# A float32 mixture-of-experts tail on one core: the second gather moved into its own position, the last group moved behind the branch, and two gathers done in four column groups

## The chip, the cores and the metric

One core of a Trainium2 chip runs the whole program, one launch. The metric is the device time of one execution in microseconds, as the median of the runs; lower is better. Everything is computed in float32 (the matmuls of the expert part are plain float32).

## The reference, cut to what matters

Two layers of a diffusion backbone over 256 latent and 256 context tokens of width 1024. The last sub-layer of the second layer is the part at issue: a mixture of eight experts, each token using the best two.

```python
logits = (hf @ w_r).astype(jnp.float32) + b_r          # hf: 256 tokens x 1024
top_v, top_i = lax.top_k(logits, TOP_K)                # TOP_K = 2 of 8
gates = jax.nn.softmax(top_v, axis=-1)
combine = jnp.sum(one_hot(top_i, N_EXPERTS) * gates[..., None], axis=-2)
for e in range(N_EXPERTS):                             # w1, w3: 1024 x 2816, w2: 2816 x 1024
    out = out + combine[:, e:e + 1] * ((silu(hf @ w1[e]) * (hf @ w3[e])) @ w2[e])
```

Then comes the residual and a final RMSNorm.

## The kernel before, in words

**Positions, steps and units.** The eight experts are handled one after the other, in eight positions. Position 0 always holds expert 0; the others are filled with experts by their number of tokens, so which expert's weights a position loads is read from a register (line 588). Positions 1, 3, 5 and 7 (SMALL) work on two blocks of 32 token slots, the others on three. Each position is three steps (CH = 3, `g = 3 * e + j`), which cover 1024, 1024 and 768 of the 2816 hidden columns; there are NG = 24 steps. In step g TensorE does four pairs of first products (`pair(g, p)`, line 1172: two of the eight k tiles each, line 1187 issues the matmuls), turns the activations of step g-1 (`turn`, line 1158, lines 1164 and 1169) after its first pair, and ends with the second products of step g-1 (`second_unit`, line 1121, lines 1145 and 1153), one for each 256 hidden rows. The 32 token slots of a block are the columns of the loaded operand, so four such matmuls stand side by side in the array (four column groups of 32).

**The weight ring.** SyncE issues one DMA for each unit of weights, in the order in which TensorE uses them (lines 568 to 606, the DMA is line 575): a unit is 1 MB, or 768 KB for the first products of the third step of a position. The ring holds 16 units. Unit v is issued once `unit_done` says that unit v-16 has been used; a pair releases its two units with its last matmuls, each second product releases one. TensorE waits on a unit's arrival (`landed_unit`, line 1076).

**Gathers.** Before a position can run, the rows of its tokens are picked out of the 256 token rows `h2_rows` by products with 0/1 matrices that VectorE writes (`select`, line 2193). `gather(r, turn, i_, ps)` (line 1079, matmuls on line 1088) does one call: for turns 0 and 1 two k tiles, 96 slots each, two matmuls each with a full 128x128 loaded operand, so four matmuls a call and four calls a turn. ScalarE copies each call's bank to `held` (`gathered_rows`, line 1628, the copy is line 1633). Turn 0 serves position 0, turn 1 position 1, turn 2 positions 2 and 3, turn 3 the rest. Turn 0's four calls run back to back ahead of step 0 (lines 1197 and 1198). FILL_STEPS (line 71) says where the calls of the others go: turn 1's after the pairs (1,0), (1,1), (2,0) and (2,1), so inside position 0, turn 2's and turn 3's inside positions 1 and 3. In step 3 (ROW_STEP), the first of position 1, TensorE also turns the residual rows (`gate_rows`, `residual_rows`, lines 1092 to 1105), one after each pair, and VectorE copies them out (`rows_copied`, line 2233).

**The branch.** All of this is round 0. At its end every engine reads the largest number of tokens of an expert and branches (`rounds`, lines 534 to 547): only if some expert has more than 96 tokens do further rounds run. In TensorE's program the branch stands after the second products of step 22; behind it `last_scatter` (line 1238) does the three second products of step 23 and the scatter to token order (line 1118), and then VectorE and ScalarE do the final norm and SyncE stores.

```python
v = UNITS * r + H_UNIT[g, p, m]
load(v, unit(v, w), of_expert(name, e)...)      # unit v waits for unit_done >= v - 15
```

Of the kernel before, what the change touches and what calls it, by code (L numbers as in the profile page):

```python
# [11 lines left out]
P = 128  # L12
D = 1024
KT = D // P
# [44 lines left out]
CH = 3  # L59
WIDTH = [1024, 1024, 768]  # L60
NG = NE * CH
# [6 lines left out]
PLACE = [3, 4, 5, 6, 1, 2, 3, 0]  # L68
GATHERS = [(0,), (1,), (2, 3), (7, 4, 5, 6)]
FILL_ROWS = [2, 2, 2, 1]  # L70
FILL_STEPS = [None, [(1, 0), (1, 1), (2, 0), (2, 1)], [(4, 0), (4, 1), (5, 0), (5, 1)],
              [(g, p) for g in (10, 11) for p in range(4)]]
FIRST_FILL = [0, 4, 8, 12]
FILLS = 21
# [62 lines left out]
def backbone(nc, t, out):  # L137
    with ExitStack() as ctx:
# [46 lines left out]
        bank = [ctx.enter_context(nc.psum_tensor(f"bank{i}", [P, 512], F32)) for i in range(8)]  # L185
# [319 lines left out]
        def fill_of(turn, i, r):  # L505

            return FILLS * r + FIRST_FILL[turn] + i

        def fills_at(g, spot):

            return [(turn, FILL_STEPS[turn].index((g, spot))) for turn in (1, 2, 3) if (g, spot) in FILL_STEPS[turn]]

        def fill_sums(g, spot):

# [1 line left out]

        FIRST_FILL_BANK = [7, 6, 5, 3]
        ROW_STEP = CH
        ROW_BANK = [5, 2, 5, 2, 5]
        SCATTER_BANK = [0, 1, 2, 5]  # L520

        def kept_before(i, r):
# [98 lines left out]
        def _(pe):  # L621
# [457 lines left out]
            def gather(r, turn, i_, ps):  # L1079

                pe.wait_ge(sel_ready, SELECTS * r + turn + 1)
                cols = C * len(GATHERS[turn])
                for c in range(FILL_ROWS[turn]):
                    k = FILL_ROWS[turn] * i_ + c
                    if r + turn == 0:
                        pe.wait_ge(tok_ready, 2 if k < KT // 2 else 4)
                    for n in range(2):
                        i = mm(ps[:, c * cols:(c + 1) * cols], h2_rows[:, n, k * P:(k + 1) * P], sel_at[turn][n],
                               start=(n == 0), stop=(n == 1))
                i.then_inc(gather_mm, 1)  # L1090

            def residual_rows(pr):

                half, n = divmod(pr, 2)
                for c in range(4):
                    i = pe.transpose(bank[ROW_BANK[pr + 1]][:, c * P:(c + 1) * P], xv[:, 4 * half + c, n * P:(n + 1) * P], ident)
                i.then_inc(row_mm, 1)
# [56 lines left out]
                                   start=first, stop=last)  # L1154
                i.then_inc(unit_done, 1)

            def experts(r):
                def turn(g):

                    s01, s2 = sums(g, 0), sums(g, 1)  # L1160
                    nq = chunk_width(g) // P
                    pe.wait_ge(a_tok, before_group(g, r, 2, 3) + 2)
                    for q in range(nq):
                        i = pe.transpose(s01[:, q * P:(q + 1) * P], act_01[:, q * P:(q + 1) * P], ident)  # L1164
                    i.then_inc(a_mm, 1)
                    if g // CH not in SMALL:
                        pe.wait_ge(a_tok, before_group(g, r, 2, 3) + 3)
                        for q in range(nq):
                            i = pe.transpose(s2[:, q * HD:(q + 1) * HD], act_2[:, q * P:(q + 1) * P], ident[0:HD, 0:HD])
                        i.then_inc(a_mm, 1)  # L1170

                def pair(g, p):
                    e = g // CH
                    cw = chunk_width(g)
                    v3, v1 = UNITS * r + H_UNIT[g, p, 0], UNITS * r + H_UNIT[g, p, 1]
                    w3, w1 = unit(v3, 2 * cw), unit(v1, 2 * cw)
                    landed_unit(v3)
                    landed_unit(v1)
                    for kk in range(2):
                        k = 2 * p + kk  # L1180
                        for b in BLOCK_ORDER[e]:
                            ps = sums(g, b)
                            last = b == BLOCK_ORDER[e][-1]
                            for job in range(4):
                                w = w1 if (job < 2) == (b == 1) else w3
                                a = job % 2
                                i = mm(ps[BLOCK * job:BLOCK * (job + 1), 0:cw], gathered_block(e, k, b),  # L1187
                                       w[:, kk, a * cw:(a + 1) * cw], start=(k == 0), stop=(k == KT - 1))
                                if kk == 1 and last and a == 1:
                                    i.then_inc(unit_done, 1)  # L1190
                            if k == KT - 1 and not last:
                                i.then_inc(h_done, 1)

                if r:
                    pe.wait_ge(yt_ready, before(0, r, 1, 2))
                    pe.wait_ge(scatter_added, 4 * r)
                for i_ in range(4):
                    gather(r, 0, i_, bank[FIRST_FILL_BANK[i_]])
                for g in range(NG):
                    e, j = divmod(g, CH)  # L1200
                    for turn_ in (1, 2, 3):
                        if g in [step + 1 for step, _ in FILL_STEPS[turn_]]:
                            done = [step < g for step, _ in FILL_STEPS[turn_]].count(True)
                            pe.wait_ge(gathered, fill_of(turn_, done, r))
                    if g == 1 and r == 0:
                        pe.wait_ge(pos_ready, 2)
                    if g == ROW_STEP + 1 and r == 0:
                        pe.wait_ge(row_copied, 5)
                    if g == NG - 1:
                        pe.wait_ge(gathered, FILLS * (r + 1))  # L1210
                    for p in range(KT // 2):
                        if g == 0:
                            pe.wait_ge(gathered, fill_of(0, p + 1, r))
                        pair(g, p)
                        if g and p == 0:
                            turn(g - 1)
                        if g == ROW_STEP and r == 0:
                            if p == 0:
                                pe.wait_ge(L[1]["x1"], KT)
                                gate_rows()  # L1220
                            else:
                                pe.wait_ge(row_copied, p)
                            residual_rows(p)
                        for turn_, k in fills_at(g, p):
                            if p == 1 and (g - 1) // CH not in SMALL:
                                pe.wait_ge(a_t2, before_group(g - 1, r, 0, 1) + 1)
                            if p >= 2:
                                pe.wait_ge(gathered, fill_of(turn_, k - 1, r))
                            gather(r, turn_, k, fill_sums(g, p))
                        if g == NG - 2 and p == 2:  # L1230
                            slots_of_tokens(r, sums(g - 1, 2))
                    if g:
                        for u in range(ROW_UNITS[(g - 1) % CH]):
                            if g == NG - 1 and u == 2:
                                turn(g)
                            second_unit(r, g - 1, u)

            def last_scatter(r, last):
                for u in range(ROW_UNITS[CH - 1]):
                    second_unit(r, NG - 1, u)  # L1240
                pe.wait_ge(yt_ready, before(0, r + 1, 1, 2))
                for n in range(2):
                    scatter(n)
# [18 lines left out]
        def _(act):  # L1262
# [364 lines left out]
            def experts(r):  # L1627
# [20 lines left out]
                def first_turned(g):  # L1648
                    cw = chunk_width(g)
                    act.wait_ge(a_mm, before_group(g, r, 1, 2) + 1)  # L1650
                    f(turned(g)[0][:, 0:cw], sums(g, 0)[:, 0:cw], ACT.Copy).then_inc(a_t01, 1)  # L1651
# [14 lines left out]
                for g in range(NG):  # L1666
                    e, j = divmod(g, CH)
                    if e and j == 1 and e - 1 not in SMALL:
                        rows_shifted(e - 1)
                    if g:  # L1670
                        first_turned(g - 1)
                    if e and j == 1:
                        rows_kept_of(e - 1, r)
                    for p in range(KT // 2):
                        for turn_, k in fills_at(g, p):
                            gathered_rows(turn_, k, fill_sums(g, p))
                    if g == NG - 2:
                        act.wait_ge(gather_mm, FILLS * (r + 1))
                        f(held[:, 4864:5120], sums(g - 1, 2)[:, 0:2 * P], ACT.Copy).then_inc(gathered, 1)
                    gated(g)  # L1680
                first_turned(NG - 1)

            def last_rows(r, last):
# [671 lines left out]
```

## Time and profile before

| what | value |
| --- | --- |
| median of 3 runs | 1497.35 us (1496.7 to 1498.34) |
| the profiled execution | 1495.29 us |
| its span in the profile | 1493.5 us |
| TensorE busy | 1385.8 us, 93% |
| TensorE's mean granted clock | 0.977 of full |
| weight DMAs of the experts | 216 of 1024 KB and 64 of 768 KB |
| HBM read, over the span | 390.76 MB, 264 GB/s |

The span runs from the first to the last instruction of the profiled execution; 1.8 us of its own time lie outside it. TensorE's busy share is high everywhere, and the DMA share is low in the first half (the dense layers) and near full in the second (the experts), so the two halves have different limits, and a share over the whole span says little. PE in rows is TensorE's matmuls, PEld its loads of the stationary operand. A float32 matmul of the code leaves two records in the trace. The clock is the granted share of 2.4 GHz: 1.00 is 2.4 GHz, 0.50 is 1.2 GHz.

### The profile page before, as it was taken

The numbers are of one execution on the slowest core, as the hardware profiler recorded it, in microseconds if no ns is written. First come the engines' busy times: TensorE is split into PE (matmuls) and PEld (weight loads), VectorE is DVE, ScalarE is ACT, GpSimd is POOL, SyncE is SP. The second block draws the span as 40 slices with busy tenths as digits, with TensorE's granted clock in tenths as the row PEclk, the third lists the DMA queues.
The fourth block names the chain that finished last, engine by engine and source line by source line (L and its number), as shares of the span: only waits on it lengthen the run. The fifth ranks groups of instructions, "written<-read, shape, count | busy, mean of one in ns | idle before, by whom it ended". The sixth has DMA issues, their size and how long they took to land.

```text
span 1493.5 us, 25370 instructions
## 1 busy us (share of the span) xinstructions
PE 1385.8 (93%) x11135; PEld 822.5 (55%) x11135; DVE 525.5 (35%) x954; ACT 398.7 (27%) x701; POOL 4.1 (0%) x8
## 2 busy tenths in 40 slices
PE   6899889999999999989798999999999997799865
PEld 3688558888888888878584343333332332233221
DVE  2799885422232333579953102011100001001112
ACT  3522484522222222475562101010110000001001
POOL 0000000000000000000000000000000000000010
PEclk9899999999999999999999999999999999999998
DMA  9997903533231142510526899999999999999995
GB/s 351 385 337 276 347 1 113 170 113 100 70 113 57 43 182 86 189 41 25 197 113 261 320 400 406 409 408 407 409 406 409 406 409 408 408 409 402 409 407 202
DMA packets 147029, 395.89 MB, mean 265 GB/s; under 512 B 7488, under 2 KB 38752, under 8 KB 146912
## 3 DMA queue, kind: packets, MB, share of 16 engines
q1 hardware_dynamic: 144000, 388.86, 68.5%
q10 hardware_dynamic: 2336, 3.24, 0.6%
q8 instruction: 90, 1.47, 0.4%
q0 software_dynamic: 576, 2.10, 0.4%
q14 instruction: 27, 0.22, 0.0%
HBM read 390.76 MB, written 3.41 MB: 264 GB/s over the span
## 4 chain that ended last, share of the span: by engine, by line
PE 73%; DMA 13%; DVE 6%; SPq 6%; ACT 1%; issue 1%; DVEq 0%; ACTq 0%
PE bank L1187 20%; DMA weight_ring<-in_exp_w 10%; PE bank L1145 7%; PE bank L1012 5%; PE bank L1011 5%; PE bank L1010 5%; SPq L575 4%; PE bank L733 4%; PE bank L734 4%; PE bank L735 3%; PE bank L1019 3%; PE bank L1021 3%; PE bank L1020 3%; PE bank L679 2%; PE bank L1153 2%; DMA weight_ring<-in_w_ada 2%
## 5 line engine op out<-in xcount | busy, mean ns | idle before, releaser
L1187 PE MATMUL bank<-weight_ring,gathered 128*32 128x512 f32 (+1 forms) x3840 | 397.7, 565 | 33.0 <-DMA weight_ring<-in_exp_w 33.0
L1187 PEld LDWEIGHTS bank<-weight_ring,gathered 128*32 128x32 f32 x3840 | 125.9, 111 | 282.1 <-issue 281.1
L2226 DVE TENSOR_TENSOR scratch<-scratch,bank 64x512 f32<-64x512 f32 (+1 forms) x60 | 38.4, 639 | 399.8 <-ACT scratch L1646 397.2
L1145 PE MATMUL bank<-weight_ring,scratch 128*32 128x512 f32 x1360 | 162.4, 598 | 9.0 <-DMA weight_ring<-in_exp_w 8.8
L1012 PE MATMUL bank<-slot_halves,slot_halves 128*128 128x512 f32 x336 | 130.9, 390 | 0.0
L1011 PE MATMUL bank<-hT_halves,slot_halves 128*128 128x512 f32 x336 | 130.9, 390 | 0.0
L1010 PE MATMUL bank<-slot_halves 128*128 128x512 f32 x320 | 124.7, 390 | 0.0
L734 PE MATMUL bank<-hT_halves,slot_halves 128*128 128x512 f32 (+1 forms) x352 | 122.2, 347 | 0.0
L1832 DVE SCALAR_TENSOR_TENSOR weight_ring<-scratch,conv_weights,weight_ring 128x512 f32<-128x512 f32 (+1 forms) x207 | 121.3, 637 | 2.6 <-ACT weight_ring L1427 0.7
L733 PE MATMUL bank<-slot_halves,slot_halves 128*128 128x512 f32 (+1 forms) x284 | 106.0, 373 | 8.6 <-DVE slot_halves L1739 5.7
L1145 PEld LDWEIGHTS bank<-weight_ring,scratch 128*32 128x32 f32 x1360 | 43.7, 111 | 112.1 <-issue 91.5
L1646 ACT ACTIVATE scratch<-bank 64x512 f32<-64x512 f32 (+1 forms) x60 | 33.4, 556 | 230.3 <-PE bank L1187 229.4
L735 PE MATMUL bank<-slot_halves,slot_halves 128*128 128x512 f32 (+1 forms) x256 | 91.5, 357 | 0.0
L1749 DVE TENSOR_TENSOR slot_halves<-weight_ring,slot_halves 128x1024 fp32r<-128x1024 f32 x44 | 53.8, 1226 | 106.9 <-ACT slot_halves L1387 106.9
L1651 ACT ACTIVATE scratch<-bank 128x512 f32<-128x512 f32 (+1 forms) x23 | 13.0, 565 | 259.7 <-PE bank L1164 259.7
L734 PEld LDWEIGHTS bank<-hT_halves,slot_halves 128*128 128x128 f32 x352 | 68.6, 195 | 7.5
L1011 PEld LDWEIGHTS bank<-hT_halves,slot_halves 128*128 128x128 f32 x336 | 63.1, 188 | 13.2
L1012 PEld LDWEIGHTS bank<-slot_halves,slot_halves 128*128 128x128 f32 x336 | 63.1, 188 | 13.0
L1019 PE MATMUL bank<-slot_halves,slot_halves 128*128 128x512 f32 x176 | 68.7, 390 | 0.3 <-DVE tail_halves L1755 0.3
L1387 ACT ACTIVATE slot_halves<-weight_ring 128x1024 fp32r<-128x1024 f32 x44 | 46.3, 1056 | 79.2 <-PE bank L1012 77.9
L1010 PEld LDWEIGHTS bank<-slot_halves 128*128 128x128 f32 x320 | 60.1, 188 | 12.4
L733 PEld LDWEIGHTS bank<-slot_halves,slot_halves 128*128 128x128 f32 x284 | 55.4, 195 | 18.0 <-DVE slot_halves L1739 5.8
(301 smaller groups left out, 1576.0 us busy)
## 6 DMA issues: line engine op xcount, KB each, us to landing
weight_ring<-in_exp_w SPq DMA_DIRECT2D x216, 1024.0 KB, 18.3
weight_ring<-in_w_ada SPq DMA_DIRECT2D x24, 2048.0 KB, 14.0
weight_ring<-in_exp_w SPq DMA_DIRECT2D x64, 768.0 KB, 15.6
weight_ring<-in_ffn_w SPq DMA_DIRECT2D x33, 1024.0 KB, 5.5
weight_ring<-in_w_in SPq DMA_DIRECT2D x8, 1024.0 KB, 11.6
weight_ring<-in_w_out SPq DMA_DIRECT2D x4, 2048.0 KB, 11.5
weight_ring<-in_w_in SPq DMA_DIRECT2D x2, 3072.0 KB, 15.4
expert_rows<-scratch ACTq DMA_DIRECT2D x14, 128.0 KB, 6.0
```

The lines of the kernel that those rows point to most:

```text
L575: sp.dma_start(dst, src).then_inc(unit_in[v % UNITS_HELD], 16)
L733: mm(ps, hi, x[l][k][:, 0:T], start=(k == 0), stop=False)
L734: mm(ps, hi, x_lo[k][:, 0:T], start=False, stop=False)
L735: return mm(ps, lo, x[l][k][:, 0:T], start=False, stop=(k == KT - 1))
L1010: mm(b, hi, h_hi[k], start=(k == 0), stop=False)
L1011: mm(b, hi, h_lo[k], start=False, stop=False)
L1012: i = mm(b, lo, h_hi[k], start=False, stop=(k == KT - 1))
L1019: mm(b, hi, a_hi[n % 2], start=(n == 0), stop=False)
L1145: i = mm(bank[6][quarter, :], at01[:, c0:c0 + BLOCK], w2[:, i_, half * 512:(half + 1) * 512], start=(first and i_ == 0), stop=(last and i_ ...
L1187: i = mm(ps[BLOCK * job:BLOCK * (job + 1), 0:cw], gathered_block(e, k, b), w[:, kk, a * cw:(a + 1) * cw], start=(k == 0), stop=(k == KT - 1))
L1749: tt(piece(h, True), piece(h), piece_head(h).bitcast(F32), ALU.subtract).then_inc(lo_ready, 1)
L1832: i = stt(out=dst, in0=src, scalar=wk, in1=dst, op0=ALU.mult, op1=ALU.add)
```

## The change

Turn 1's four gather calls leave position 0: the first goes after the last pair of step 2, the other three ahead of the pairs (3,0), (3,1) and (3,2), all into bank 5. Of turn 0's calls two stay ahead of pair (0,0), the third and fourth go after pairs (0,0) and (0,1). For both turns each full-width matmul becomes four, on 32 columns of the loaded operand each, into four partition groups of the bank. In step 3 the residual rows come out of bank 2 in place of banks 2 and 5 in turn, each a pair later but the last. Step 23 (its four pairs, the turns of steps 22 and 23, the second products of step 22) is now issued inside each arm of TensorE's branch instead of ahead of it; the other engines' branches stay where they were. ScalarE's copies follow the calls.

```diff
-FILL_STEPS = [None, [(1, 0), (1, 1), (2, 0), (2, 1)], [(4, 0), (4, 1), (5, 0), (5, 1)],
+FILL_STEPS = [None, None, [(4, 0), (4, 1), (5, 0), (5, 1)],
               [(g, p) for g in (10, 11) for p in range(4)]]
...
-        ROW_BANK = [5, 2, 5, 2, 5]
+        ROW_BANK = [2, 2, 2, 2, 5]
+        NEXT_FILL_BANK = 5
...
-                    for n in range(2):
-                        i = mm(ps[:, c * cols:(c + 1) * cols], h2_rows[:, n, k * P:(k + 1) * P], sel_at[turn][n],
-                               start=(n == 0), stop=(n == 1))
+                    if turn < 2:
+                        for n in range(2):
+                            for q in range(4):
+                                i = mm(ps[32 * q:32 * q + 32, c * cols:(c + 1) * cols],
+                                       h2_rows[:, n, k * P + 32 * q:k * P + 32 * q + 32], sel_at[turn][n],
+                                       start=(n == 0), stop=(n == 1))
+                    else:
...
-            def experts(r):
+            def expert_steps(r, begin, end):
...
-                for i_ in range(4):
-                    gather(r, 0, i_, bank[FIRST_FILL_BANK[i_]])
-                for g in range(NG):
+                if begin == 0:
+                    gather(r, 0, 0, bank[FIRST_FILL_BANK[0]])
+                    gather(r, 0, 1, bank[FIRST_FILL_BANK[1]])
+                    if r == 0:
+                        pe.wait_ge(tok_ready, 4)
+                for g in range(begin, end):
...
                         if g == 0:
                             pe.wait_ge(gathered, fill_of(0, p + 1, r))
+                        if g == CH:
+                            pe.wait_ge(gathered, fill_of(1, p + 1, r))
+                            if p < 3:
+                                gather(r, 1, p + 1, bank[NEXT_FILL_BANK])
                         pair(g, p)
+                        if g == CH - 1 and p == KT // 2 - 1:
+                            gather(r, 1, 0, bank[NEXT_FILL_BANK])
+                        if g == 0 and p < 2:
+                            gather(r, 0, p + 2, bank[FIRST_FILL_BANK[p + 2]])
...
                                 pe.wait_ge(row_copied, p)
-                            residual_rows(p)
+                                residual_rows(p - 1)
+                            if p == KT // 2 - 1:
+                                residual_rows(p)
...
+            def experts(r):
+                expert_steps(r, 0, NG - 1)
+
             def last_scatter(r, last):
+                expert_steps(r, NG - 1, NG)
                 for u in range(ROW_UNITS[CH - 1]):
                     second_unit(r, NG - 1, u)
...
+                    if g == CH:
+                        gathered_rows(1, 1, bank[NEXT_FILL_BANK])
                     if g:
                         first_turned(g - 1)
+                    if g == CH:
+                        gathered_rows(1, 2, bank[NEXT_FILL_BANK])
+                        gathered_rows(1, 3, bank[NEXT_FILL_BANK])
...
                     gated(g)
+                    if g == CH - 1:
+                        gathered_rows(1, 0, bank[NEXT_FILL_BANK])
```

## Rows read from the trace of the kernel before

**Rows 1.** The page: mean DMA share and rate in 40 equal slices.
```profile
DMA  9997903533231142510526899999999999999995
GB/s 351 385 337 276 347 1 113 170 113 100 70 113 57 43 182 86 189 41 25 197 113 261 320 400 406 409 408 407 409 406 409 406 409 408 408 409 402 409 407 202
```
**Rows 2.** Busy time by stretch of the expert part (us; busy, records; clock, DMA share, GB/s).
```profile
798.00:808.00 10.00, 10.00 (x80) 6.62 (x83) 5.75 (x31) 1.32 (x4) 0.00 (x0) 0.83 0.02 5
808.00:848.00 40.00, 40.00 (x372) 13.57 (x368) 3.39 (x6) 5.50 (x9) 0.00 (x0) 1.00 0.82 299
848.00:1455.00 607.00, 567.46 (x5295) 193.11 (x5291) 67.33 (x127) 53.45 (x98) 3.88 (x4) 0.99 1.03 407
...
803.00:1085.00 282.00, 282.00 (x2662) 98.90 (x2664) 35.70 (x83) 28.90 (x53) 0.00 (x0) 1.00 0.98 384
```
**Rows 3.** Waits (us, times, longest): SyncE's queue in 798:1085, TensorE in 1085:1470.
```profile
SPq L575 <- PE bank L1187: 119.9, 30, 22.3
...
PE bank L1187 <- DMA weight_ring<-in_exp_w: 33.0, 24, 3.3
```
**Rows 4.** Weight DMAs, issue and landing: those running in 843:844, then all of 870:1455.
```profile
L575 SPq DMA_DIRECT2D weight_ring<-in_exp_w x2: 368/442/515, 842.8 to 843.2; - x2
...
DMA to landing us min/median/max: 5.0/6.1/7.1
...
DMA to landing us min/median/max: 6.9/18.3/24.3
```
**Rows 5.** Timeline at the first gather, and the clock over 799:803.
```profile
797.78 5.44 PE L1088 MATMUL bank<-xT,scratch 128*128 128x96 f32 x32 [0.37 <-DVE xT L2207]
798.95 0.33 ACT L1633 ACTIVATE gathered<-bank 128x192 f32<-128x192 f32 x1 [1.87 <-PE bank L1088]
803.15 25.96 PE L1187 MATMUL bank<-weight_ring,gathered 128*32 128x512 f32 x240
...
799.00:803.00 4.00, 4.00 (x24) 4.00 (x22) 3.54 (x18) 0.94 (x3) 0.00 (x0) 0.57 0.00 0
```
**Rows 6.** Timeline of TensorE in step 1, around turn 1's second call.
```profile
831.08 5.36 PE L1187 MATMUL bank<-weight_ring,gathered 128*32 128x512 f32 x48
836.36 0.97 PEld L1088 LDWEIGHTS bank<-xT,scratch 128*128 128x128 f32 x8 [0.84 <-issue]
837.43 10.08 PE L1187 MATMUL bank<-weight_ring,gathered 128*32 128x512 f32 x92
```
**Rows 7.** Timeline of TensorE at other products in 32-column groups.
```profile
123.59 0.43 PE L821 MATMUL bank<-scratch,constants 128*32 128x128 f32 x8
123.95 0.66 PE L688 MATMUL bank<-constants,weight_ring 128*128 128x128 f32 x4
124.53 3.70 PE L679 MATMUL bank<-weight_ring,silu_c 128*32 128x128 f32 x128
128.16 0.50 PE L733 MATMUL bank<-slot_halves,slot_halves 128*128 128x512 f32 x1
```
**Rows 8.** The end: timeline, chain, last weight DMA, and clocks by stretch.
```profile
1445.70 2.79 PE L1187 MATMUL bank<-weight_ring,gathered 128*32 128x384 f32 x32 [2.08 <-DMA weight_ring<-in_exp_w]
...
1468.68 1.28 ACT L1284 ACT_TABLE_LOAD   x1 [3.28 <-issue]
...
1474.92 7.17 PE L1145 MATMUL bank<-weight_ring,gathered 128*32 128x512 f32 x48 [5.45 <-issue]
...
1471.38 3.54 issue
...
L575 SPq DMA_DIRECT2D weight_ring<-in_exp_w x1: 2204/2204/2204, 1457.0 to 1457.0; - x1
...
DMA to landing us min/median/max: 20.6/20.6/20.6
...
1434.00:1437.00 3.00, 2.17 (x12) 0.60 (x16) 0.00 (x0) 0.00 (x0) 0.00 (x0) 0.54 1.01 402
...
1475.00:1478.00 3.00, 3.00 (x16) 0.79 (x20) 0.00 (x0) 0.00 (x0) 0.00 (x0) 0.50 0.13 46
```

More of the change, by code:

```diff
@@ L509, in fills_at @@
         def fills_at(g, spot):
-            return [(turn, FILL_STEPS[turn].index((g, spot))) for turn in (1, 2, 3) if (g, spot) in FILL_STEPS[turn]]
+            return [(turn, FILL_STEPS[turn].index((g, spot))) for turn in (2, 3) if (g, spot) in FILL_STEPS[turn]]
         def fill_sums(g, spot):
@@ L1086, in gather @@
                         pe.wait_ge(tok_ready, 2 if k < KT // 2 else 4)
-                    for n in range(2):
-                        i = mm(ps[:, c * cols:(c + 1) * cols], h2_rows[:, n, k * P:(k + 1) * P], sel_at[turn][n],
-                               start=(n == 0), stop=(n == 1))
+                    if turn < 2:
[5 more added lines that the diff above has]
+                    else:
+                        for n in range(2):
+                            i = mm(ps[:, c * cols:(c + 1) * cols], h2_rows[:, n, k * P:(k + 1) * P], sel_at[turn][n],
+                                   start=(n == 0), stop=(n == 1))
                 i.then_inc(gather_mm, 1)
@@ L1192, in pair @@
                                 i.then_inc(h_done, 1)
-                if r:
+                if r and begin == 0:
                     pe.wait_ge(yt_ready, before(0, r, 1, 2))
                     pe.wait_ge(scatter_added, 4 * r)
-                for i_ in range(4):
-                    gather(r, 0, i_, bank[FIRST_FILL_BANK[i_]])
-                for g in range(NG):
+                if begin == 0:
[4 more added lines that the diff above has]
+                for g in range(begin, end):
                     e, j = divmod(g, CH)
-                    for turn_ in (1, 2, 3):
+                    for turn_ in (2, 3):
                         if g in [step + 1 for step, _ in FILL_STEPS[turn_]]:
```

## The prediction

> **What bounds the kernel now.** I read the page's slices first [rows 1]. The first half is not touched by the change; the expert part is slices 21 to 39, and there the DMA share stands at 9 and the rate at about 408 GB/s. The reader is to see two things: the full rate holds for some 600 us, and just ahead of it there is a ramp (261, 320, 400). The stretches [rows 2] sharpen that. From 848 to 1455 the DMA engines never rest (share 1.03, 407 GB/s). From 798 to 808 they move nothing, and from 808 to 848 only 299 GB/s. Meanwhile TensorE is busy without a break from 803 to 1085. The waits [rows 3] say why: SyncE waited 119.9 us for the products of line 1187 to release ring units, and only after 1085 does TensorE itself wait for weights (24 times, 33.0 us). So in position 0 TensorE holds the DMAs back, and from 848 on the DMAs set the pace until the last unit lands. The issue rows fix the changeover [rows 4]. The pair of units issued at 842.8 and 843.2 landed after 5.0 and 7.1 us, as two transfers do that find idle engines: 2 MB at 407 GB/s is 5.15 us, and some 2 us of latency. After 870 no unit landed in under 6.9 us and the median is 18.3 us: there is a queue. The last starved units are thus those that pair (1,2) released, and **every microsecond by which that release comes sooner moves the whole DMA stream behind it**. The end is the second place. The last unit lands at 1457.0 + 20.6 = 1477.6 [rows 8], but TensorE had stood still for 5.45 us before 1474.92 with no releaser, although the unit that it needed first had landed at 1471.38 (the chain shows 3.54 us of issue). That is the branch. On top, the clock is at 0.50 (1.2 GHz) from 1475 to 1478, so the first of the three remaining units takes 3.4 us instead of 1.7.
>
> **The change, part by part.**
>
> *Turn 0.* Today its 32 records run from 797.78 to 803.15, 5.37 us [rows 5]. The new form has 32 records a call instead of 8, on 32 columns. The nearest row is the modulation product in 32-column groups with 128 moving columns: 128 records from 124.53 to 128.16, 28.4 ns each [rows 7]. With 96 moving columns a record costs between 96/128 of that and the same, so a call is 0.68 to 0.91 us; I take 0.80, since short products rarely scale fully. The slow end is the 8 records that took 0.36 us to the next start, 45 ns each [rows 7], so 1.44 us. Two calls put the first pair at 799.4; ScalarE's copy of the first call (it began 1.2 us after that call's start and took 0.33) is done by then, and the fourth token-row copy was already done before the gather began. The clock stays as it was: over 799 to 803 it was 0.57, which withholds 4 x 0.43 = 1.7 us of full-clock work. Pair (0,0), 5.15 us at full clock (48 of the 107 ns records that 240 in 25.9 us give [rows 5]), then ends at 799.4 + 5.15 + 1.7 = 806.3 instead of 808.3, and the two calls now behind pairs (0,0) and (0,1) take 1.6 us back. With c for a call, the release is early by 5.37 - 1.72 - 4c = 3.65 - 4c: 0.45 us at c = 0.80.
>
> *Turn 1 out of position 0.* Pair (1,1) starts at 831.08 and pair (1,2) at 837.43, after the call between them [rows 6]: 6.35 us for a pair of 5.15, so a call costs 1.20 us there, 0.2 of it the change of shape around it. Two such calls lie ahead of the release by pair (1,2). That is 2.4 us, and with 0.45 the stream of DMAs moves forward by 2.85 us. The next two calls, in step 2, also go; they no longer count, as the queue has formed.
>
> *Turn 1 in its new place.* Four calls, 3.2 us, between 872 and 900. They cost nothing, because the queued DMAs cover them: units issued after 870 landed 6.9 us or more after issue, mostly 12 and later 18 [rows 4], and TensorE comes there 5 us sooner than today. Its net lead after step 3 is 2.85 + 2.4 - 3.2 = 2.0 us against the DMAs' 2.85, so the queue gets 0.8 us shorter, far less than it holds. Were that cover gone, they would cost their 3.2 us. Each call waits only for the copy of the one before it, a pair or a second product earlier. ScalarE's new waits stand ahead of the turn of step 2, whose products come after pair (3,0), so nobody is queued behind them in vain. The residual rows all from bank 2 need a 0.7 us copy by VectorE within a pair of 3.4 us; two copies instead of one then follow the last pair, and 7.7 us of second products cover them. SyncE's and GpSimd's queues pass nothing new.
>
> *The branch.* It moves to 1443.6, where TensorE waits 2.08 us for weights anyway [rows 8]. With the same 5.45 us it restarts at 1449.1 instead of 1445.7, at half clock for some 3.7 us as after 1474.92, which withholds 1.85 us. All units of pairs (23,0) and (23,1) are there by then, so TensorE runs without waits: four pairs of 2.6, two turns with their gaps of 1.4, four second products of 1.7 and the lost 1.85 end at about 1469.8, against 1469.5 today. The unit it needs next comes at 1471.38. So the branch is free there, with 1.6 us to spare, and 4.5 us before it touches the last product. Every weight DMA of step 23 waits for products that stand ahead of the branch, so the stop holds no DMA back. The last unit, landed at 1477.6, is used up 1.72 us later, and with 0.25 us of latency VectorE goes on at 1479.6 instead of 1482.15: 2.5 us.
>
> The Trainium skill ("Runtime: NRT & Kernel Launch", instruction fetch mechanics) says that a taken branch to code not yet fetched must first load it by DMA. The 5.45 us agree. By that rule the new place, with the DMA share at 1.03, could be dearer than the old one; ScalarE's branch at 1465.4, also at a full share, took only 3.28 us [rows 8], which speaks against it.
>
> **Sum:** 2.85 + 2.5 = 5.35 us, in general 8.55 - 4c. The profiled execution took 1495.29 us, of which the span is 1493.5, and would take 1489.9. It lies 2.06 us under the median of 1497.35, and I carry that over: **1492.0 us**.
>
> **The rivals.**
> 1. *The end gives less* (chance 0.17). TensorE now waits 1.4 to 1.7 us before each of the last three products. A stop of 2.9 us brought half clock at 1434 [rows 8], one of 2.08 us did not. If the clock falls all the same, the last product takes 3.4 us instead of 1.7: gain 2.85 + 0.8, 1493.7 us. A branch of 11 to 12 us does the same. For it speaks that the engine is at work little more than half the time there.
> 2. *The front gives nothing* (0.13): the clock after 799 stays low for longer because the new calls are short, or the slowest of the DMA engines had a queue already. Only the 2.5 us of the end remain, 1494.85 us. Against it: the units issued at 842.8 landed as on idle engines [rows 4].
> 3. *Slower* (0.05): the narrow loads do not run beside the products. A call is then 32 loads of 0.11 us, c = 3.5, and 8.55 - 14 = -5.5 us: 1502.9 us. The place is turn 0, the point of no gain is c = 2.14 us. Against it stand the 28.4 ns a record, load and product together, of [rows 7]. The Trainium skill ("TensorE: Matmul & The Clock Gate", the mechanism of packing small matmuls) has loads overlap products only in other row groups, which column groups are not; this trace does not bear that out.
> 4. *Neither part moves the end* (0.05), because the branch grows by some 10 us beside a loaded DMA: 1497.3 us.
>
> **How the numbers follow.** The forecast as it stands has 0.60, and lies between 1490.0 (c = 0.68, and a clock that recovers sooner) and 1493.9 (c = 1.2). A difference of 0.2%, 3 us, is about what measurements of this kernel can tell from none. Faster by more than that, under 1494.4 us: 0.59 of the forecast, 0.12 of rival 1 and 0.04 of rival 2, 0.75. Slower by more: rival 3 and a very long branch, 0.05. The rest, 0.20, is the same. The range of 1490.0 to 1495.8 takes in rivals 1 and 2.
>
> **What would show it.** Right: pair (0,0) begins near 799.4; a gather call spans some 0.8 us; the units that pair (1,2) releases are issued near 840.0; TensorE's gap of some 5.5 us stands near 1441 and not before the last three products; those start as their units land, the last at about 1474.8; the clock stays at 1.00 there; the span ends near 1488.2. Wrong: calls of 1.2 us or more, first weight issues no sooner than 808, a DMA share under 1 anywhere from 850 to 1450, or TensorE restarting after 1455 behind the branch.

## The result, and the profile after

The changed kernel takes 1488.8 us (median of 6 runs, 1486.87 to 1491.72); the kernel before took 1497.82 us beside it. The ratio is 0.9943, with a 95% interval of 0.9931 to 0.9954: 8.5 us faster, clear of what this measurement can tell from none. The forecast was 1492.0 us, 5.35 us faster, and its range ended at 1490.0. The sign was right, the size too small by some 3 us.

Two profiled executions can't be subtracted as they stand. The profiled one of the changed kernel took 1491.72 us, the slowest of its six, and it was late before the change had any say: its first gather product begins at 801.40, that of the kernel before at 797.78 [rows 5]. Over the profiles of this study that moment lies anywhere from 797.7 to 802.0, whatever the kernel, as the dense half is not equally long each time. So I count from it. Call the start of the first gather product zero; "the end" is the start of VectorE's scaling of the last rows (line 2125 before, 2157 after), behind which everything takes 11.3 us in every profile.

| from the first gather product, us | before | changed | changed, second profile |
| --- | --- | --- | --- |
| units that pair (1,2) released are issued | 45.0 | 40.1 | 40.1 |
| last unit issued | 659.2 | 655.4 | 654.4 |
| last unit landed | 679.8 | 673.3 | 672.3 |
| the end | 684.4 | 677.2 | 674.5 |

The stretches answer to [rows 2], with the columns as there: the clock, the DMA share and the rate stand last.

```profile
808.00:848.00 40.00, 40.00 (x428) 14.60 (x424) 4.72 (x9) 6.10 (x10) 0.00 (x0) 1.00 0.87 312
848.00:1455.00 607.00, 561.72 (x5335) 191.21 (x5329) 66.24 (x126) 52.99 (x98) 3.88 (x4) 0.98 1.03 407
803.00:1085.00 282.00, 282.00 (x2824) 100.70 (x2817) 38.92 (x100) 29.59 (x55) 0.00 (x0) 1.00 0.99 387
```

The picture is the old one: TensorE busy without a break to 1085, the DMA engines at 1.03 from 848 on. Only the ramp is better, 312 GB/s instead of 299, although this execution came 3.6 us later. Nowhere behind it does the DMA share fall: what the ramp gained was kept.

TensorE's timeline at the first gather, and the clock there, for [rows 5] and [rows 6]:

```profile
801.40 1.53 PE L1091 MATMUL bank<-xT,scratch 128*32 128x96 f32 x64 [0.38 <-DVE xT L2239]
802.33 0.33 ACT L1658 ACTIVATE gathered<-bank 128x192 f32<-128x192 f32 x1 [1.64 <-PE bank L1091]
802.76 5.36 PE L1195 MATMUL bank<-weight_ring,gathered 128*32 128x512 f32 x48
807.91 0.87 PE L1091 MATMUL bank<-xT,scratch 128*32 128x96 f32 x32
808.57 5.36 PE L1195 MATMUL bank<-weight_ring,gathered 128*32 128x512 f32 x48
...
829.97 0.66 PE L1172 MATMUL bank<-constants,scratch 128*128 128x128 f32 x4
830.56 0.46 PE L1177 MATMUL bank<-constants,scratch 64*128 64x64 f32 x4
830.95 15.66 PE L1195 MATMUL bank<-weight_ring,gathered 128*32 128x512 f32 x144
...
802.60:806.60 4.00, 4.00 (x52) 1.55 (x48) 3.52 (x18) 0.40 (x2) 0.00 (x0) 1.00 0.02 4
```

The reader is to see three things. A call takes 807.91 to 808.57, **0.66 us** (20.6 ns a record, less than the 21.3 ns by which I had bounded it, and no gap for a change of shape). Pair (0,0), the four pairs of step 0 being named (0,0) to (0,3), begins 1.36 us after the gather and takes 5.15 us. And the clock is **1.00** in the very stretch, 1.2 to 5.2 us behind the first gather product, in which it was 0.57 before [rows 5].

The end, TensorE's timeline and the last unit, for [rows 8]:

```profile
1440.10 2.54 PE L1153 MATMUL bank<-weight_ring,scratch 128*32 128x512 f32 x16 [0.26 <-DMA weight_ring<-in_exp_w]
1448.85 3.49 PE L1195 MATMUL bank<-weight_ring,gathered 128*32 128x384 f32 x20 [6.21 <-issue]
1454.38 2.16 PE L1195 MATMUL bank<-weight_ring,gathered 128*32 128x384 f32 x12 [2.04 <-issue]
1456.47 1.12 PE L1172 MATMUL bank<-constants,scratch 128*128 128x128 f32 x4
1457.52 8.38 PE L1195 MATMUL bank<-weight_ring,gathered 128*32 128x384 f32 x96
1465.73 3.61 PE L1153 MATMUL bank<-weight_ring,scratch 128*32 128x512 f32 x32
1469.27 0.55 PE L1172 MATMUL bank<-constants,scratch 128*128 128x128 f32 x3
1469.75 3.64 PE L1153 MATMUL bank<-weight_ring,scratch 128*32 128x512 f32 x32
1473.20 5.33 PE L1153 MATMUL bank<-weight_ring,gathered 128*32 128x512 f32 x48
...
L576 SPq DMA_DIRECT2D weight_ring<-in_exp_w x1: 2232/2232/2232, 1456.8 to 1456.8; - x1
...
DMA to landing us min/median/max: 17.9/17.9/17.9
```

The stop at the branch is where it was forecast, but it is 6.21 us, and 20 records later there is a second one of 2.04 us that nothing had announced. Behind the second stop TensorE runs without one wait for weights; the last unit landed at 1456.8 + 17.9 = 1474.7 and its product began at 1476.6. So in this execution the end was TensorE's own, by 1.9 us.

### The profile page after: what moved, and what is told of

The parts are those of the page before. It is cut to its first block, busy times and chain, and to the rows that moved or that the text cites. A ratio compares the mean times of both kernels' runs of the same rounds, so it can differ in the third digit from the quotient of the medians.

```text
span 1489.9 us, 25756 instructions
## 1 busy us (share of the span) xinstructions
PE 1385.7 (93%) x11327; PEld 824.0 (55%) x11327; DVE 525.8 (35%) x954; ACT 398.9 (27%) x701; POOL 4.1 (0%) x8
## 4 chain that ended last, share of the span: by engine, by line
PE 77%; DMA 11%; DVE 6%; SPq 3%; ACT 2%; issue 1%; DVEq 0%; ACTq 0%
PE bank L1195 22%; DMA weight_ring<-in_exp_w 9%; PE bank L1153 7%; PE bank L1011 5%; PE bank L1012 5%; PE bank L1013 5%; PE bank L734 4%; PE bank L735 4%; PE bank L736 4%; PE bank L1020 3%; PE bank L1022 3%; PE bank L1021 3%; PE bank L680 2%; DMA weight_ring<-in_w_ada 2%; SPq L576 2%; PE bank L1161 2%
```

## The experiments

Each kernel ran beside the kernel before on the same chip; a ratio below is to that, with its 95% interval, and a gain in us is worked out from it. Numbers from a profile count from the first gather product unless they are times of the trace.

### Parts of the change alone

**Column groups alone.** In the kernel before:

```diff
+                    if turn < 2:
+                        for n in range(2):
+                            for q in range(4):
+                                i = mm(ps[32 * q:32 * q + 32, c * cols:(c + 1) * cols],
+                                       h2_rows[:, n, k * P + 32 * q:k * P + 32 * q + 32], sel_at[turn][n],
+                                       start=(n == 0), stop=(n == 1))
...
```

> The kernel before with one edit: the calls of turns 0 and 1 in four column groups, in their old places, branch as before. Theory A (the front gain is the sum of call prices ahead of the release by pair (1,2), and a call in column groups takes 0.66 us, as in the changed kernel's trace, against 1.06 to 1.34 in full width): six calls count, so 2.7 us faster, up to 3.8 where the low clock of before fell on the gather, 1494 to 1495 us. Theory B (the column groups are worth nothing by themselves, the gain is the move): within 1 us of the kernel before. In the trace: turn 0 takes 2.7 us under A at full clock.

1494.13 us, ratio 0.9981 (0.9972 to 0.9990): 2.8 us. Turn 0's four calls took 2.67 us, the clock did not fall (1.00 where it was 0.57), and the last unit landed at 675.6 instead of 679.8. Theory A holds; theory B, that the form of the products is worth nothing by itself, does not. Not all of the front's gain got through, though:

```profile
799.72 2.85 PE L1090 MATMUL bank<-xT,scratch 128*32 128x96 f32 x128 [0.37 <-DVE xT L2214]
802.39 26.74 PE L1194 MATMUL bank<-weight_ring,gathered 128*32 128x512 f32 x240
829.06 0.66 PE L1171 MATMUL bank<-constants,scratch 128*128 128x128 f32 x4
```

The 240 records of the five pairs behind the gather took 0.8 us more than before (26.74 against 25.96 us [rows 5]). So of the 2.7 us by which turn 0 got shorter 1.9 reach the turn of step 0, and the release by pair (1,2) is 2.9 us early. What holds the pairs up behind four column-group calls in a row was not tried; in the changed kernel, with two, they take 5.15 us each.

**Moves alone.** The changed kernel with these two edits undone:

```diff
-                    if turn < 2:
-                        for n in range(2):
-                            for q in range(4):
...
-                    else:
-                        for n in range(2):
...
+                    for n in range(2):
+                        i = mm(ps[:, c * cols:(c + 1) * cols], h2_rows[:, n, k * P:(k + 1) * P], sel_at[turn][n],
+                               start=(n == 0), stop=(n == 1))
...
-                expert_steps(r, 0, NG - 1)
+                expert_steps(r, 0, NG)
...
-                expert_steps(r, NG - 1, NG)
```

> The changed kernel with full-width gather products and the branch in its old place: only the places of the calls differ from the kernel before. Theory A: two calls of 1.2 us leave the stretch ahead of pair (1,2), four changes of array shape of 0.2 us come in, so 2.0 us faster, 1495 to 1496 us. Theory B (the move is the whole front gain): 5 us faster, 1493 us.

1496.46 us, ratio 0.9992 (0.9983 to 1.0001): 1.2 us, at the edge of what can be told from none. Theory B falls. The median is below the 2.0 us of theory A, whose value the interval still takes in, and in the profile the last unit is issued 1.4 us earlier than before. The timeline shows one reason:

```profile
801.95 2.16 PE L1089 MATMUL bank<-xT,scratch 128*128 128x96 f32 x16 [0.37 <-DVE xT L2231]
804.04 6.86 PE L1188 MATMUL bank<-weight_ring,gathered 128*32 128x512 f32 x48
810.83 1.13 PE L1089 MATMUL bank<-xT,scratch 128*128 128x96 f32 x8
...
803.20:807.20 4.00, 4.00 (x23) 1.47 (x26) 3.52 (x19) 0.58 (x2) 0.00 (x0) 0.57 0.01 4
```

The clock falls again, 1.6 to 1.8 us behind the first gather product as in the kernel before, and now the fall lies on pair (0,0), which takes 6.8 us instead of 5.15. The gather in full width, whose loads took 0.97 us of a call's 1.06 [rows 6], lost 1.1 us to it (5.37 us for four calls, against 4.24 at 1.06 a call); a pair loses 1.6.

**The branch alone.** The kernel before with `experts` cut in two as in the change.

> The kernel before with step 23 moved behind TensorE's branch and nothing else. As predicted: the branch of 5.5 us lies in a wait, TensorE waits for each of the last three units again and the gain is 2.5 us. Rival, from the changed kernel's trace: the branch costs 6.2 us, a second stop of 2 us follows and half clock too, so TensorE runs without any wait from there to its last product, 36 us later; the end is then TensorE's and not the last unit's; gain again about 2.5 us, but with no wait for weights in the last 20 us, and the last unit lands over 3 us before its product ends. Time 1494.5 to 1495.5 us under both.

1494.03 us, ratio 0.9976 (0.9968 to 0.9985): 3.6 us, with an interval that takes in the 2.5 forecast. Its profile, of one of the slower of its 12 executions, shows neither the first text's course nor the rival's:

```profile
1452.09 5.23 PE L1187 MATMUL bank<-weight_ring,gathered 128*32 128x384 f32 x32 [5.36 <-issue]
...
1473.07 1.92 PE L1145 MATMUL bank<-weight_ring,gathered 128*32 128x512 f32 x16
1475.48 1.92 PE L1145 MATMUL bank<-weight_ring,gathered 128*32 128x512 f32 x16 [0.49 <-DMA weight_ring<-in_exp_w]
1480.47 3.22 PE L1145 MATMUL bank<-weight_ring,gathered 128*32 128x512 f32 x16 [3.06 <-DMA weight_ring<-in_exp_w]
```

One stop of 5.36 us, no second one, and TensorE has caught up by 1473. But the last unit was late (20.4 us from issue to landing), TensorE waited 3.06 us for it, and then the clock fell and its product took 3.2 us. That is rival 1 of the prediction, seen once; in this execution the branch gave 0.7 us, in the median 3.6.

**Both gather edits, branch as before.**

> The changed kernel with TensorE's branch back in its old place. Theory A: the weight stream is 3.4 us early, 5.1 where the low clock falls before the gather and not into it; nothing at the end: 1492.5 to 1494.5 us, and with the branch move's 2.5 us this adds up to the changed kernel. Theory C (the end gives most of the surplus, as the load of the final norm's gain no longer competes with the last weights): only 2.9 us faster, 1494.9 us.

1492.26 us, ratio 0.9964 (0.9950 to 0.9978): 5.4 us. With the branch's 3.6 that makes 9.0, the changed kernel's 8.5 within the intervals. Theory C (most of the surplus is made at the end) falls: the last unit landed at 673.6, 6.2 us early, with the branch in its old place. Against the sum of the two edits alone, 2.8 + 1.2, the pair gives 1.4 more, which the three intervals don't tell from none. In the profiles the release by pair (1,2) is 2.9, 1.6 and 4.9 us early, so there the surplus is 0.4.

### The clock at the gather

**Turn 0 in full width again**, turn 1 in column groups (`if turn == 1:` in place of `if turn < 2:`).

> The changed kernel with turn 0 in full width again; turn 1 stays in column groups. Theory A (the column-group gather keeps TensorE's clock up where the full-width one lets it fall): about 1.2 us after the first gather product begins, the granted clock falls to 0.50 for some 3 us again, 1.7 us of work, and four calls are 0.4 to 0.6 us dearer: 3.3 to 4 us slower than the changed kernel's 1488.8 us. Theory B (the fall that was missing is chance): no fall here either, or one in some runs only, and 1.6 to 2.2 us slower.

1492.77 us, ratio 0.9972 (0.9963 to 0.9981): 4.0 us slower than the changed kernel's 1488.8, and 4.7 than the next kernel, which ran beside it. The clock over the same 4 us is 0.57 again:

```profile
800.41 2.19 PE L1096 MATMUL bank<-xT,scratch 128*128 128x96 f32 x16 [0.37 <-DVE xT L2239]
802.53 6.83 PE L1195 MATMUL bank<-weight_ring,gathered 128*32 128x512 f32 x48
...
801.60:805.60 4.00, 4.00 (x24) 1.56 (x27) 3.52 (x19) 0.64 (x2) 0.00 (x0) 0.57 0.02 4
```

**Turn 1 in full width again** (`if turn == 0:`).

> The changed kernel with turn 1 in full width again, in its new places. Theory A (queued weights cover turn 1 in position 1, so the form of its products is worth nothing there): within 0.7 us of the changed kernel's 1488.8 us. Rival (TensorE's time counts there too): four calls at 0.4 to 0.6 us dearer, 2 us slower, 1491 us.

1488.11 us, ratio 0.9940 (0.9927 to 0.9954): no difference to the changed kernel. In position 1 the queued weights cover the calls, so the form of their products costs nothing, as the prediction had it. The clock did not fall.

**One call in full width.** The changed kernel with only turn 0's first call, or only its second (`(0, 1)` in place of `(0, 0)`), in full width:

```diff
-                    if turn < 2:
+                    if turn < 2 and (turn, i_) != (0, 0):
```

> The changed kernel with only turn 0's first call in full width (1.06 us in place of 0.66). Theory A1 (what decides is how TensorE is at work in the first microsecond of the gather, up to the point where the full-width gather saw the clock fall): the clock falls to 0.50 again, 1.7 + 0.5 us slower than the changed kernel, 1491 us. Theory A2 (the second call in column groups and the pair behind it are enough): no fall, 0.5 us slower.

> The changed kernel with only turn 0's second call in full width. Under A1 the column-group call ahead of it is enough: no fall, 0.5 us slower than the changed kernel, 1489.3 us. If a full-width call anywhere ahead of the first pair brings the fall: 1491 us, with the clock at 0.50 for 3 us.

1489.28 us, ratio 0.9945 (0.9930 to 0.9960), and 1489.15 us, ratio 0.9947 (0.9932 to 0.9962). The clock stayed at 1.00 in both:

```profile
799.85 1.13 PE L1096 MATMUL bank<-xT,scratch 128*128 128x96 f32 x8 [0.37 <-DVE xT L2239]
800.91 0.87 PE L1091 MATMUL bank<-xT,scratch 128*32 128x96 f32 x32
801.60 5.33 PE L1195 MATMUL bank<-weight_ring,gathered 128*32 128x512 f32 x48
...
801.05:805.05 4.00, 4.00 (x68) 1.61 (x66) 3.52 (x18) 0.63 (x2) 0.00 (x0) 1.00 0.00 0
```

So A1 falls, A2 stands: either of the two calls ahead of the first pair in column groups is enough. Over all profiles the count is clean. With all calls ahead of the first pair in full width, two or four (the kernel before, moves alone, branch alone, turn 0 in full width, and the kernel before with an early load, below), the clock fell 1.6 to 1.8 us behind the gather's start, five times of five; with one or more in column groups it never did, in eleven profiles. Nor is it that the dense pairs begin sooner: in the kernel with column groups alone the first pair began 2.67 us behind the gather's start, later than the 2.09 us of the moves alone, and the clock stayed. What happened ahead of it was the same in all: about 8.5 us before the gather the clock had fallen once already, in the router's short products, and had come back. Why one form lets it fall and the other doesn't, these runs don't show.

### The end

**The branch ahead of step 21.** In the changed kernel:

```diff
-                expert_steps(r, 0, NG - 1)
+                expert_steps(r, 0, NG - CH)
...
-                expert_steps(r, NG - 1, NG)
+                expert_steps(r, NG - CH, NG)
```

> The changed kernel with TensorE's branch ahead of step 21 in place of step 23, so the whole last position stands in the arms. Theory A (in the changed kernel the end is TensorE's, still catching up after the stop of 6.2 us, the second stop of 2 us and the half clock): TensorE waits for each of the last three units again, the end is the last landing plus 2 us, 0.6 to 1.9 us faster than the changed kernel: 1487 to 1488.2 us. Rival (then TensorE waits for the last unit, the clock falls in that wait as in the branch-only kernel, and its product takes 3.2 us): no faster, 1488.8 us or a little slower.

1488.53 us, ratio 0.9948 (0.9934 to 0.9962): no difference in the timed runs. In the profile theory A's course is there (a stop of 4.5 us at the branch, 0.5 us more in step 21, then a wait for each of the last three units, 0.66, 0.49 and 1.81 us, the end at 675.3, 2.0 us behind the last landing), but it buys nothing, because the last unit landed later after its issue, 19.2 instead of 17.9 us.

**The same, and the gain's load early.**

```diff
+                if r == 0:
+                    act.wait_ge(L[1]["wo_mm"], KT)
+                    act.dma_start(final_b, ...).then_inc(final_in, 16)
                 for i_ in range(4):
                     gathered_rows(0, i_, bank[FIRST_FILL_BANK[i_]])
...
-                    act.dma_start(final_b, ...).then_inc(final_in, 16)
```

> As the kernel with the branch ahead of step 21, and the 512 KB load of the final norm's gain is issued at the start of the expert part, where the DMA engines stand idle, in place of the end. Theory A (that load shares the DMA engines with the last weights, 1.3 us of them at 407 GB/s): the last unit lands 673 us or less after the first gather product, 0 to 1.3 us faster than with the branch ahead of step 21 alone: 1486 to 1487.5 us. Rival: the last unit's landing does not depend on it, no difference.

1486.31 us, ratio 0.9934 (0.9921 to 0.9948). The last unit landed 17.9 us after issue, at 671.9, and the wait for it was 0.56 us instead of 1.81. I ran this kernel and the changed one again, side by side:

> The changed kernel once more, for a second profile of its end and on the same chip as the next. The first profile had a second stop of 2.04 us behind the branch, which three kernels with the same branch did not have. Expected: one stop of 4.5 to 5.5 us at the branch, no second one, the last three units each waited for, the end 676.2 us after the first gather product, 1488 us. Rival: the second stop belongs to this program, and comes again.

> The kernel with the branch ahead of step 21 and the gain's load at the start of the expert part once more, against the changed kernel on one chip. Its last unit landed 671.8 us after the first gather product against 674.1 in the kernel with turn 1 in full width, so 2.3 us faster than the changed kernel: 1486 us. If only chips differed: no difference.

The changed kernel: 1487.34 us, ratio 0.9932 (0.9919 to 0.9946). The other: 1487.7 us, ratio 0.9928 (0.9913 to 0.9943). **No difference**, so the 2.3 us that I had expected of it are not there. The changed kernel's second profile says why. Its end:

```profile
1436.61 5.39 PE L1153 MATMUL bank<-weight_ring,scratch 128*32 128x512 f32 x32 [2.40 <-DMA weight_ring<-in_exp_w]
1446.83 4.06 PE L1195 MATMUL bank<-weight_ring,gathered 128*32 128x384 f32 x20 [4.83 <-issue]
1452.37 1.48 PE L1195 MATMUL bank<-weight_ring,gathered 128*32 128x384 f32 x12 [1.49 <-issue]
...
1469.62 5.33 PE L1153 MATMUL bank<-weight_ring,gathered 128*32 128x512 f32 x48
...
L576 SPq DMA_DIRECT2D weight_ring<-in_exp_w x1: 2230/2230/2230, 1454.9 to 1454.9; - x1
...
DMA to landing us min/median/max: 17.9/17.9/17.9
```

The second stop is there again (1.49 us; the rival of that text holds, my expectation does not), TensorE again runs through to the end, and yet the end comes 2.2 us behind the last landing, 674.5. The two stops delay TensorE, and with it ScalarE, which issues the gain's 512 KB load only when step 23 has been turned: 669.2 us after the gather's start, where it was 666.8 in the kernel with turn 1 in full width, which has one stop. By then the last unit is nearly in and lands 1.3 us sooner. The stops cost about as much as they give back.

**The gain's load early, nothing else.** In the kernel before and in the changed one:

> The kernel before with the 512 KB load of the final norm's gain moved from the end to the start of the expert part, nothing else. Theory G (that load shares the DMA engines with the last weights and delays the last unit): the last unit lands 2.7 us after less of its issue, 17.9 in place of 20.6 us, and the time falls by up to 2.7 us, 1494.5 to 1496 us; what is left of it behind the branch is less, as the first of the three units then lies ready for longer. Rival: the last landing was late for another reason, 20.6 us stays, no difference.

> The changed kernel with the gain's load at the start of the expert part. Theory G: in the changed kernel the load comes too late to disturb the last unit (17.9 us from issue to landing already), so nothing is left to gain: within 0.7 us of the changed kernel, the last landing at 17.9 us after issue. Rival (the load at the end costs its 1.3 us in every kernel): 1.3 us faster.

1497.04 us, ratio 1.0006 (0.9997 to 1.0015), and 1488.29 us, ratio 0.9947 (0.9933 to 0.9961). In the kernel before the last unit landed 19.5 instead of 20.6 us after issue, so in these two profiles the load delayed it, but the time did not move: the end there is not that unit's.

```profile
1477.34 7.38 PE L1145 MATMUL bank<-weight_ring,gathered 128*32 128x512 f32 x48 [5.36 <-issue]
```

TensorE restarts behind the branch at 1477.34 and runs its 48 records in one piece, the last unit (landed at 1459.5 + 19.5 = 1479.0) long there when its turn comes. In the changed kernel nothing was left to gain, as theory G said.

## Why the prediction was wrong in size

**What bounds the kernel, and that the release by pair (1,2) sets the DMA stream: right.** The units that it releases were issued at 45.0 before and 40.1 after, 4.9 us sooner, and the last unit of all was issued 4.8 us sooner in the changed kernel's second profile. There the whole lead passed through 600 us of full DMA share without loss; in the first profile, with 3.8 us at the last unit, 1.1 us of it went lost, for a reason that wasn't looked for. The DMA share stayed at 1.03 although four calls were added in positions 0 and 1 behind the release, and the form of turn 1's calls moved nothing (1488.11 us): the cover held.

**The term of turn 0 was mis-sized**, and it is the step that failed: "The clock stays as it was: over 799 to 803 it was 0.57, which withholds 4 x 0.43 = 1.7 us of full-clock work". The clock did not stay low there: it was 1.00 in the changed kernel. I had taken the fall for a feature of the moment; it went with the work then done. Both calls ahead of the first pair in full width bring it, one in column groups prevents it. Those 1.7 us are the largest piece of the error. The second is the price of a call: 0.66 us instead of 0.80. I had held the exact ratio of moving columns to be the floor and gone above it; the 96-column records came out at it, so four calls are 0.56 us cheaper. With both, turn 0 gives 5.37 - 4 x 0.66 = 2.7 us instead of 0.45. Turn 1's two calls were taken a little too dear: the first stands behind a turn, which is in full width too, and costs 1.06 us and not 1.20, so together they give 2.3 us instead of 2.4. That makes 5.0 us, where the trace has the release 4.9 us early. The range's lower end allowed for c = 0.68, but only a little for the clock, and rival 2 took the clock to be able to get worse alone. The other end was added up wrongly: at c = 1.2 the sum gives 1493.6 us, not 1493.9. Nothing hangs on it.

**The end: 2.5 us forecast, 2.4 measured, by another course.** From the last landing to the end it was 4.6 us before and is 2.2 in the changed kernel's second profile. But the forecast had TensorE wait for each of the last three units. In both profiles of the changed kernel it waits for none: the branch costs 4.8 to 6.2 us, and a second stop of 1.5 to 2.0 us follows, which I had not foreseen. The five kernels with the branch in the same place and fewer gather instructions ahead of it (branch alone; turn 0, turn 1, the first or the second call in full width) have no second stop; the kernel with it ahead of step 21 has one of 0.5 us. So it goes with the program's place, not with the weights; what makes it was not tried. The DMA rows offer a candidate. In the first profile the instruction queue moves 0.02 MB between 1451.8 and 1454.4, beside the second stop, and the second profile shows the same between 1449.5 and 1452.4. In the kernel with turn 1 in full width such a transfer runs between 1447.5 and 1450, about as soon behind the first stop, and TensorE doesn't stand still. The second stop may thus be TensorE reaching instructions that are not there yet; no run tests that. Rival 1 (the clock falls in the wait for the last unit) was seen once, in the branch-only kernel, and never in the changed one.

**One gain had no term.** The last unit landed 20.6 us after issue before, 17.9 in the changed kernel. Of these 2.7 us, 1.3 are the gain's load (the 512 KB that ScalarE loads for the final norm). In the seven kernels with column-group calls that issue it 11 to 12 us behind the last unit's issue that unit took 19.2 us; in the changed kernel's two profiles, with 15 to 17 us between the two, and in the three kernels that issue it at the start of the expert part it took 17.9. Once TensorE no longer stands at the branch, the last landing is what the end hangs on, and so they count. The other 1.4 us (19.5 us in the kernel before even without that load) stay open. With the load in place the last unit took 20.4 us with the branch alone moved, 19.5 with the moves alone and 19.2 with the column groups alone, so they go with the gathers and not with the branch. Together: 4.8 + 2.7 + 2.4 = 9.9 us between the first profile of before and the second of the changed kernel, where the timed runs say 8.5 and 10.2; the first profile of the changed kernel had the longest stops of all and made 7.2.

**Rivals 3 and 4** did not come. Loads in column groups run beside the products: 32 loads of 0.11 us each pass in a call of 0.66 us, 20.6 ns a record. The rule that the Trainium skill ("TensorE: Matmul & The Clock Gate", the mechanism of packing small matmuls) gives, that loads overlap products only in other row groups, doesn't hold in this trace. And the branch beside a loaded DMA cost 4.5 to 6.2 us against the 5.45 of before, and not some 10 us more.

## What to carry to other kernels

- Where a ring of buffers is refilled by a saturated queue, find the last moment at which the queue ran dry: what the releasing engine saved ahead of it was kept to the end here (4.9 us), and what it paid behind it cost nothing, as long as the queue covered it.
- A fall of TensorE's clock in a trace is not a constant to be carried over. When the change replaces the work just ahead of it, price both: the fall stays, or it goes.
- Move a branch to where its engine has slack, but look at what else the engine's delay moves. Here the delay held back a competing load, and gave back about what it cost.

## What was not expected of the hardware

- Behind the start of a gather in full width, four calls or two and then a pair, the granted clock fell from 2.4 to 1.2 GHz after 1.6 to 1.8 us, for 3.4 us, in five profiles of five. With the same products in column groups, even only half of those ahead of the first pair, it stayed at 2.4 GHz in eleven of eleven.
- The same call costs 1.06 us in full width (8 records) and 0.66 us in four column groups (32 records), and 1.20 us in full width where it stands between column-group products [rows 6].
- The end of the same code with the same branch has one stop of 4.5 us or two of 4.8 and 1.5 us. Which of them comes went with how many instructions stand ahead of it.
